# A three-branch diffusion layer: the first Hyena fold moved ahead of the pooling averages, and attention computed on negated scores with a fused add-and-minimum

## The reference

```python
# neighbourhood attention, one head: q_rot, k_rot are rotated; bias holds a learned table and -1e30 outside the window
s_lat = einsum(q_rot, k_rot) * dh**-0.5 + bias
s_ctx = einsum(q_plain, k_ctx) * dh**-0.5
p = softmax(concatenate([s_lat, s_ctx], -1))
out = p_lat @ v + p_ctx @ v_ctx

# pooling: windows of 2, 4, 8, 16 tokens, 128 channels each
y_pool = (mean over the window - u) @ pool_w[g] * pool_scale

# Hyena, order 2: v, x1, x2 come from a 3-tap convolution
z = v
for o, gate in enumerate((x1, x2)):
    z = gate * (irfft(rfft(z) * h_spec[o]) + z * skip[o])
```

## Time and profile before

| | |
|---|---|
| time, 3 runs | 1544.64 us median, 1544.02 to 1546.52 |
| profiled execution | 1546.05 us, its span 1544.3 us |
| PE, DVE, ACT, POOL busy | 94%, 56%, 41%, 26% of the span |
| mean granted clock of TensorE | 0.976 of full speed |
| pooling results to first transform, layer 0 / layer 1 | about 152 to 163 us / 1033 to 1050 us of the span |
| attention, layer 0 / layer 1 | about 295 to 353 us / 1123 to 1157 us of the span |

### The profile page before, as it was taken

The page is one execution under the profiler, slowest core; times in us unless marked ns, Lnnn a source line. Parts: engine busy times, 40 slices in busy tenths (PEclk is TensorE's granted clock), DMA queues, the critical chain, the costliest instruction groups (busy, mean ns, idle before and its releaser), DMA issues. The chain is left out here.

```text
span 1544.3 us, 20627 instructions
## 1 busy us (share of the span) xinstructions
PE 1447.1 (94%) x8184; PEld 1080.0 (70%) x8184; DVE 869.9 (56%) x1265; ACT 634.5 (41%) x862; POOL 404.3 (26%) x367
## 2 busy tenths in 40 slices
PE   6999999899999997899999988989988997999997
PEld 2688788557778875688888854787958995545444
DVE  7626576763223347899999956465873565111112
ACT  3432321364223225588787836432264443010102
POOL 1455443201334520111111012564305670000000
PEclk9999999999999998999999999999999999999998
DMA  9422211475544544899999986342305776899993
GB/s 361 150 82 82 83 55 63 169 273 206 172 139 141 195 174 171 302 406 418 415 414 412 402 293 246 104 150 82 103 22 175 240 259 260 340 421 421 420 421 154
DMA packets 117186, 362.78 MB, mean 235 GB/s; under 512 B 7806, under 2 KB 73664, under 8 KB 86496
## 3 DMA queue, kind: packets, MB, share of 16 engines
q1 hardware_dynamic: 109584, 334.62, 56.9%
q0 software_dynamic: 7504, 26.81, 4.7%
HBM read 349.86 MB, written 11.53 MB: 234 GB/s over the span
## 5 line engine op out<-in xcount | busy, mean ns | idle before, releaser
L911 POOL TENSOR_TENSOR w_lo<-ring,w_hi 128x256 fp32r<-128x256 f32 (+1 forms) x300 | 345.7, 1182 | 497.5 <-ACT w_hi L1962 466.0
L1101 PE MATMUL bank<-h_hi,w_hi 128*128 128x512 f32 (+1 forms) x768 | 271.5, 353 | 8.6 <-POOL w_lo L911 2.9
L1103 PE MATMUL bank<-h_lo,w_hi 128*128 128x512 f32 (+1 forms) x768 | 263.1, 343 | 0.0
L1102 PE MATMUL bank<-h_hi,w_lo 128*128 128x512 f32 (+1 forms) x768 | 263.1, 343 | 0.0
L1101 PEld LDWEIGHTS bank<-h_hi,w_hi 128*128 128x128 f32 x768 | 146.6, 191 | 35.6 <-issue 9.5
L1102 PEld LDWEIGHTS bank<-h_hi,w_lo 128*128 128x128 f32 x768 | 146.7, 191 | 17.2 <-issue 1.4
L1103 PEld LDWEIGHTS bank<-h_lo,w_hi 128*128 128x128 f32 x768 | 146.5, 191 | 16.8
L1101 PE MATMUL bank<-w_hi,h_hi 128*128 128x512 f32 (+1 forms) x384 | 140.2, 365 | 7.1 <-DVE h_lo L2911 3.1
L1962 ACT ACTIVATE w_hi<-ring 128x1024 fp32r<-128x1024 f32 x120 | 125.3, 1053 | 43.5 <-PE bank L1101 29.8
L1103 PE MATMUL bank<-w_lo,h_hi 128*128 128x512 f32 (+1 forms) x384 | 136.9, 356 | 0.0
L1102 PE MATMUL bank<-w_hi,h_lo 128*128 128x512 f32 (+1 forms) x384 | 136.8, 356 | 0.0
(11 more groups left out here) (369 smaller groups left out, 2835.8 us busy)
## 6 DMA issues: line engine op xcount, KB each, us to landing
ring<-in_w_in SPq DMA_DIRECT2D x52, 1024.0 KB, 5.3
mix<-in_w_gate_e SPq DMA_DIRECT2D x40, 1024.0 KB, 8.2
ring<-in_w_up_e SPq DMA_DIRECT2D x38, 1024.0 KB, 8.1
mix<-in_w_down_e SPq DMA_DIRECT2D x25, 1024.0 KB, 8.3
ring<-in_w_down_e SPq DMA_DIRECT2D x23, 1024.0 KB, 8.1
ring<-in_w_mod SPq DMA_DIRECT2D x19, 1024.0 KB, 5.6
operands_plain<-in_w_up_e SPq DMA_DIRECT2D x16, 1024.0 KB, 12.6
operands_plain<-in_w_down_e SPq DMA_DIRECT2D x16, 1024.0 KB, 15.8
```

The lines of the kernel that those rows point to most:

```text
L911: last = pool.tensor_tensor(w_lo[:, slot, k:k + n], rview(raw, 8)[:, k:k + n, x * P:(x + 1) * P], w_hi[:, slot, k:k + n].bitcast(F32), ALU ...
L1101: first = mm(dst, stat[0], mov[0], start=start, stop=False)
L1102: mm(dst, stat[1], mov[0], start=False, stop=False)
L1103: return first, mm(dst, stat[0], mov[1], start=False, stop=stop)
```

## The change

Two edits that don't touch each other.

1. *First fold.* DVE does fold 0 as soon as the convolutions are finished, before the pooling averages, into the buffer `ahead` (idle then) in place of `work`. PE transposes it before the pooling matmuls. ACT scales three pooling results, waits for the end of the averages (`zt` lies over their scratch), copies the transposes to `zt`, and then scales the fourth result. PE waits for each pooling result only before the transform matmul that overwrites its bank. The later folds stay where they were.
2. *Attention.* Queries are scaled by `-DH ** -0.5`, the mask is +1e30 and the bias is turned (mask minus bias), so all scores have the opposite sign; the exponential gets `scale=-1.0`. The stabiliser is then the minimum of the negated scores. For a latent unit DVE first takes the minimum of the 256 context scores of both heads, then one instruction for each head adds the bias to the 256 latent scores in place and carries the minimum on, starting from the context minimum. Context units keep one reduction, now a minimum.

```diff
@@ views
-        hy_f = work[:, 3072:4096].rearrange("p (i c u) -> p i c u", i=2, c=BK)
+        def hy_f(n):
+            v = ahead[:, 0:1024] if n == 0 else work[:, 3072:4096]
+            return v.rearrange("p (i c u) -> p i c u", i=2, c=BK)
@@ PE
                 fill_steps(plan[0])
+                def fold_transposed(n):
+                    pe.wait_ge(y_fo[l], 8 * l + 2 * n + 2)
+                    for j in range(2):
+                        for c in range(BK):
+                            last = tp(bank[4 + j][:, c * P:(c + 1) * P], hy_f(n)[:, j, c, :], ident)
+                        last.then_inc(y_tp[l], 1)
+                fold_transposed(0)
                 for c in range(BK):
                     pe.wait_ge(j_d[l], 12 + c + 1)
                     mm(bank[c][:, 0:T], poolw[:, c, :], ypool[:, c, 0:T], start=True, stop=True
                        ).then_inc(pw_pe[l], 1)
-                pe.wait_ge(pw_a[l], 4 * l + BK)
...
                         if n:
                             pe.wait_ge(y_z[l], BK * n)
-                        pe.wait_ge(y_fo[l], 8 * l + 2 * n + 2)
-                        for j in range(2):
...
+                            fold_transposed(n)
                         fill_steps(plan[3 * n + 1])
                         pe.wait_ge(y_zt[l], 8 * l + 2 * n + 2)
                         for f in (0, 2, 1, 3):
+                            if n == 0:
+                                pe.wait_ge(pw_a[l], 4 * l + f + 1)
                             mm(bank[f][:], dft_z[:, f * P:(f + 1) * P], zt[:, f // 2, :], start=True, stop=True
@@ ACT
-                            A(qT[:, g - 16, 0:T], b[:, 0:T], ACT.Copy, scale=DH ** -0.5).then_inc(j_a[l], 1)
+                            A(qT[:, g - 16, 0:T], b[:, 0:T], ACT.Copy, scale=-DH ** -0.5).then_inc(j_a[l], 1)
...
-                for c in range(BK):
+                def pool_scaled(c):
                     act.wait_ge(pw_pe[l], 4 * l + c + 1)
...
+                for c in range(BK - 1):
+                    pool_scaled(c)
                 for n in range(2 * S):
                     if n:
                         act.wait_ge(y_f[l], 16 * l + 4 * n)
+                    else:
+                        act.wait_ge(j_d[l], 12 + BK)
                     for j in range(2):
                         act.wait_ge(y_tp[l], 8 * l + 2 * n + j + 1)
                         A(zt[:, j, :], bank[4 + j][:, :], ACT.Copy).then_inc(y_zt[l], 1)
+                    if n == 0:
+                        pool_scaled(BK - 1)
                     take_tiles(taken_by(l)[n] - (0 if n else at_start))
...
-                        A(prob[:, p, 0:w], bank[p][:, 0:w], ACT.Exp, bias=pstat[:, p, 0:1],
+                        A(prob[:, p, 0:w], bank[p][:, 0:w], ACT.Exp, scale=-1.0, bias=pstat[:, p, 0:1],
@@ DVE
+                def fold(n):
...
+                    V.tensor_tensor(hy_f(n)[:, 0], late, early, ALU.add).then_inc(y_fo[l], 1)
+                    V.tensor_tensor(hy_f(n)[:, 1], late, early, ALU.subtract).then_inc(y_fo[l], 1)
+                dve.wait_ge(j_d[l], 12)
+                fold(0)
                 link(V.memset(up[:, :, 0:POOL_PAD], 0.0))
...
-                dve.wait_ge(pw_a[l], 4 * l + BK)
...
                         if n:
+                            fold(n)
                             dve.wait_ge(y_i[l], 16 * l + BK * n)
@@ DVE, mask_bias
-                    V.tensor_tensor(m, m, mask_at[l].unsqueeze(1).to_broadcast([P, 12, GRID]), ALU.add
+                    V.tensor_tensor(m, mask_at[l].unsqueeze(1).to_broadcast([P, 12, GRID]), m, ALU.subtract
@@ DVE, maxes
                     for h in range(2):
                         dve.wait_ge(a_sc[l], 2 * v + h + 1)
                         p = 2 * (v % 2) + h
-                        b = bank[p]
-                        if s == 0:
-                            k0 = 2 - 2 * x
-                            link(V.tensor_tensor(b[:, 0:SEQ].rearrange("p (s j) -> p s j", s=4),
-                                                 b[:, 0:SEQ].rearrange("p (s j) -> p s j", s=4),
-                                                 bias[:, c % 2, h, k0:k0 + 4, :], ALU.add))
                         if v >= 2:
                             dve.wait_ge(a_nm[l], 2 * (v - 2) + h + 1)
-                        V.tensor_reduce(pstat[:, p, 0:1], b[:, 0:w], AX.X, ALU.max, negate=True).then_inc(a_mx[l], 1)
+                        if s == 0:
+                            V.tensor_reduce(pstat[:, p, 3:4], bank[p][:, SEQ:NT], AX.X, ALU.min).then_inc(dve_c, 1)
+                            chain[0] += 1
+                        else:
+                            V.tensor_reduce(pstat[:, p, 0:1], bank[p][:, 0:SEQ], AX.X, ALU.min).then_inc(a_mx[l], 1)
+                    if s:
+                        return
+                    k0 = 2 - 2 * x
+                    for h in range(2):
+                        p = 2 * (v % 2) + h
+                        dve.wait_ge(dve_c, chain[0] - 1 + h)
+                        V.tensor_tensor_reduce(bank[p][:, 0:SEQ], bank[p][:, 0:SEQ],
+                                               bias[:, c % 2, h, k0:k0 + 4, :].rearrange("p s j -> p (s j)"), 1.0,
+                                               pstat[:, p, 3:4], ALU.add, ALU.min, pstat[:, p, 0:1]).then_inc(a_mx[l], 1)
```

More of the change, by code:

```diff
@@ L1316, in _ @@
                             pe.wait_ge(y_z[l], BK * n)
-                        pe.wait_ge(y_fo[l], 8 * l + 2 * n + 2)
-                        for j in range(2):
-                            for c in range(BK):
-                                last = tp(bank[4 + j][:, c * P:(c + 1) * P], hy_f[:, j, c, :], ident)
-                            last.then_inc(y_tp[l], 1)
+                            fold_transposed(n)
                         fill_steps(plan[3 * n + 1])
@@ L2521, in _ @@
                     mod_second()
+                def fold(n):
+                    s = n % S
+                    early = hv[:, :, s * SEQ + P - 1:s * SEQ - 1 if s else None:-1]
+                    late = hv[:, :, s * SEQ + P:(s + 1) * SEQ]
+                    V.tensor_tensor(hy_f(n)[:, 0], late, early, ALU.add).then_inc(y_fo[l], 1)
+                    V.tensor_tensor(hy_f(n)[:, 1], late, early, ALU.subtract).then_inc(y_fo[l], 1)
+                dve.wait_ge(j_d[l], 12)
+                fold(0)
                 link(V.memset(up[:, :, 0:POOL_PAD], 0.0))
@@ L2620, in maxes @@
                         dve.wait_ge(b_fix[l], BK * l + c + 1)
-                    w = NT if s == 0 else SEQ
                     for h in range(2):
@@ L3106, in shape_constants @@
     ok = (j[None, :] >= st[:, None]) & (j[None, :] < st[:, None] + KW)
-    c["colmask"] = np.tile(np.where(ok, 0.0, -1e30), (2, 1))
+    c["colmask"] = np.tile(np.where(ok, 0.0, 1e30), (2, 1))
     edge = np.ones((BK, 16))
```

## The result

| | median of 12 runs | range | ratio to before |
|---|---|---|---|
| before | 1543.58 us | 1539.12 to 1546.87 | |
| after | 1535.32 us | 1533.51 to 1538.62 | 0.995, 95% interval 0.9937 to 0.9962 |

That is 7.7 us less by the ratio, 5.9 to 9.7 by its interval. The profiled execution after took 1533.51 us, its span 1531.8, so 12.5 less than the span of the first profile. The profile of before shown above, at 1546.05, was near the slow end of its own spread.

A forecast was written before the change was run, and what follows sets the result against it. PE, busy 94% of the span, was taken as the bound, so its idle or slowed time counts. Gains 2.6 + 4.0 + 2.9 + 0.7 = 10.2 us from median 1544.64 gave 1534.4, range 1532 to 1536.5 (all runs 1530.0 to 1539.5).

The forecast's parts named there:

- First fold, layer 0: Pooling of layer 0: moving the fold starts the transform at 160.6, not 163.21; gain 2.6 us, bounds 1.1 and 4.4.
- First fold, layer 1: Pooling of layer 1: averages end 0.6 us later, but the chain behind them shortens; gain 4.0, bounds 0.6 and 6.0.
- Attention: Cheaper `maxes` cuts PE's waits for DVE: 2.9 us in layer 1 (bounds 0 to 3.5), 0.7 in layer 0 (0 to 1.2).
- the bound of 0.75: Attention's fused instruction, upper bound in us: 0.44 plus a read of 0.2 and a wait to drain; 0.5 was taken.
- rival 1: Clock goes another way, chance 0.18: high in layer 1 (0.11), 1532.4; drops in layer 0, low in layer 1 (0.07), 1536.7.
- rival 2: Experts of layer 0: if transfers set the pace, the 3.3 us won in layer 0 are lost; 1537.7, chance 0.08.
- rival 4: Two other rivals plus more contention in layer 1's averages: 2 to 3 us are left, 1542, chance 0.07.
- rivals 3 and 5: Attention: fused instruction saves nothing, 1538.0, chance 0.11 (3); it is slow in itself, at 1.3 us each 1551, chance 0.05 (5).
- 1.03: Attention: us per fused instruction from which the whole change was said to lose, more than twice an ordinary operation.

The follow-up runs named there:

- The doubled reductions: The kernel after, with each reduction over the 256 context scores done twice, the first into an unused column: 1540.63 us, ratio 0.9989 of before.
- the order experiment: The kernel before, with both heads' additions first, then both maxima over 512, nothing fused, old signs: 1541.68 us, ratio 0.9989 of before.

## Why the prediction was right, and where it was off

The forecast was 1534.4 with 10.2 us less; 1535.3 was measured, with 7.7 less by the ratio. Every term had the sign that it was given. That the time came out within 1 us is in part luck: the gain was put 2.5 too high, and the median of before fell by 1.1 when 12 runs had been made in place of three. By the terms of the sum:

- **First fold, layer 0: forecast 2.6, measured 2.5 between the two profiles, 2.0 on average.** The chain is as written: the step held by ACT's copy of tile 16 was to come 7.36 behind PE's first transposes and came 7.38 behind them. The experiment that moves this copy shows it. What was off is the base: the earlier trace rows show 0.54 behind the idle time of 2.27, which cost 0.9 us (122.4 against 121.5), but the clock falls there in only two of four profiles of before (0.54, 0.58, and 1.00 twice); the mean of its form is 0.5 under the first profile.
- **First fold, layer 1: forecast 4.0, measured 3.5 between the two profiles, 2.9 on average. This is the mis-sized term.** "DVE's averages end later by about 0.6": it was 1.5. The prediction counted two averages pushed behind POOL's run at half a microsecond each, which is 1.0 and was found (0.95), but put only 0.6, and it took the length of that run as given, which grew by 0.5. The run with the folds behind the second average shows that they cost about their own work, 1.3 us, at either place. The other half held: 2.76 from the averages' end to the waiting step (forecast 2.85), 5.1 from there to the spectrum (forecast 5.3, before 6.09), at a lowered clock as expected (0.56 from 1034 to 1036, 0.59 from 1036 to 1038). The rest, 0.6, is again the clock of the profile of before, whose chain was slower than that of three other profiles by 1.0.
- **Attention: forecast 2.9 and 0.7, measured 2.7 and 0.8.** The size was right, one step to it was not. The prediction has a pair of units at 6.36 on DVE against 6.24 on PE and says "So PE sets the pace"; by these numbers DVE does, by 0.12 a pair. The fused instruction was cheaper than put (0.40 from start to start, not 0.5; the bound of 0.75 has 0.11 for a wait behind the read, which no run shows: the next instruction starts together with the read, at 1121.40), and only so is a pair on DVE, 5.9, below PE's. The doubled reductions show the same limit from the other side. The earlier fall of the clock at the first scores, 0.6 between the two profiles, comes with the moved fold and is a term that the prediction put at nothing; the attention edit by itself brings layer 1 3.1 (old fold) and 3.3 (moved fold).
- **The base.** The sum was made against an execution 1.4 us above the median then known and 2.5 above the median of 12. Both fold terms were read at that execution's low clocks (0.54 from 158 to 160, 0.50 from 1040 to 1048), and this makes 1.1 of the 1.7 us that the sum has over the 8.5 above (0.5 in layer 0, 0.6 in layer 1). The other 0.6 is, nearly, the folds' delay, 0.9 more than put, less 0.3 for a chain a little shorter than put. That 8.5 and the 7.7 of the runs differ is within the interval.

The rivals. The clock did go another way, but in the kernel before (1.00 from 158 us in two of its four profiles), not after (rival 1). The gain of layer 0 was not swallowed in its experts: the stretch is as full as before and begins earlier (rival 2 falls). Layer 1's averages did end later than put, but by 1.5 and not by what would leave 2 to 3 us in all (rival 4 falls). The new `maxes` saves 0.67 a unit (rivals 3 and 5 fall): at 0.48 the fused instruction is far from 1.03. Its price stood in no row. In the trace of the kernel after a fused instruction starts 0.08 before the end of the last one (0.40 against 0.48), and the read of its accumulator, 0.14, costs nothing. Nor is a semaphore wait between two operations free: the order experiment took 0.27 us a unit out by removing such waits.

## What to carry to other kernels

Where two independent chains share an engine, put their instructions in turn, so that none waits for the one just before it; that alone was over half of what the whole edit brought to layer 1's attention (1.5 to 1.6 of 2.7 us). Making DVE faster paid there only until PE set the pace (6.24 us a pair of units against DVE's 5.9). Work moved into the stretch where POOL slowed DVE cost about its own time (1.5 us for folds of 1.3, and 1.2 behind that stretch), so count that and not only the places it takes. When a wait is removed, ask which queue was hidden behind it (here ACT's copy of tile 16, 1.53 us), and take more than one profile of the kernel before when idle times stand next to falls of the clock: the two places of the fold took 1.7 us more in one profiled execution of the same kernel than in another, and the whole took 9 us more (1548.42 against 1539.2), most of it where nothing was to be changed.

## What the runs showed of the hardware

- After the same idle time of about 2.3 us the clock of TensorE fell in two of four profiles of one kernel and stayed at 1.00 in the other two (0.54, 0.58, 1.00, 1.00 in the stretch from 158 us). In layer 1, after 2.05 us, the eight transposes took 1.94 us in three of them (0.50 from 1040 us in the first), and 1.06 in the fourth, where the clock fell only behind them (1.00 from 1036 to 1037, 0.50 from 1038).
- After 2.7 us without work the clock held for the first scores of layer 1's attention in six profiles without the moved fold (first groups 0.96 to 1.02 apart; clock 1.00 in before), and fell within them in the seven with it (1.35 to 1.86; 0.68 in after).
- The fused add-and-minimum on 128x256 float32, with one operand in PSUM, took 0.48 us, hardly more than a plain addition (0.43), and its accumulator read, 0.14 us, lay wholly under the next instruction (both from 1121.40).
- In layer 1's attention a DVE reduction that waits for the addition just before it (128x256, 0.43 long) starts 0.47 us behind that one; behind an addition that the next instruction doesn't wait for, that one starts after 0.33 (mean of two).
- A DVE fold on two SBUF operands took 0.69 us alone, and 2.92 and 2.89 us while POOL made its weight parts. The whole of DVE's work behind the last convolution was nevertheless prolonged by little more than what the folds cost alone, 1.3, at both places that were tried (25.5 and 25.2 against 24.0).
